# Sums over partitions of a matrix-vector product: eight TensorE products per group, or a transposing reduction on VectorE and four products at the end

## The reference

```python
ada = silu(c) @ w_ada + b_ada                      # (1, 1024) @ (1024, 6144)
sh_a, sc_a, g_a, sh_f, sc_f, g_f = split(ada, 6)
h = rmsnorm(x, norm_mix_w) * (1 + sc_a) + sh_a
h_res = x + g_a * token_mixer(h, ...)              # GLA + HGRN2, merged, @ w_out
h = rmsnorm(h_res, norm_ffn_w) * (1 + sc_f) + sh_f
h_res = h_res + g_f * conv_ffn(h, ...)             # @ w_up, 3-tap conv, silu*up, @ w_down
out = rmsnorm(h_res, final_norm_w)
```

## Time and profile before

| | us |
|---|---|
| median of 3 executions | 926.81 |
| lowest, highest | 925.79, 928.36 |
| the profiled execution, whole | 929.29 |
| its span, first to last instruction | 927.6 |
| TensorE busy in it | 897.6 |
| VectorE, ScalarE, GpSimd busy | 497.0, 456.5, 182.2 |

### The profile page before, as it was taken

The page is one execution under the profiler, slowest core; times in us unless marked ns, Lnnn a source line. Parts: engine busy times, 40 slices in busy tenths (PEclk is TensorE's granted clock), DMA queues, the critical chain, the costliest instruction groups (busy, mean ns, idle before and its releaser), DMA issues.

```text
span 927.6 us, 13516 instructions
## 1 busy us (share of the span) xinstructions
PE 897.6 (97%) x4828; PEld 743.4 (80%) x4828; DVE 497.0 (54%) x678; ACT 456.5 (49%) x699; POOL 182.2 (20%) x169
## 2 busy tenths in 40 slices
PE   5898999999999999999999989999999999999997
PEld 5776888888888888888887767888888888888885
DVE  2555873467634676346764357744454445623327
ACT  4475654656656565566655453533433333523224
POOL 2002253012531125311243000211112111100000
PEclk9899999999999999999999999999999999999999
DMA  9945452562425624256241940533333332232202
GB/s 326 352 141 153 118 158 64 165 182 69 115 66 160 181 68 113 78 148 184 65 128 31 203 138 10 150 90 98 105 91 90 99 104 91 98 130 90 91 0 92
DMA packets 146829, 112.16 MB, mean 121 GB/s; under 512 B 4493, under 2 KB 138137, under 8 KB 146537
## 3 DMA queue, kind: packets, MB, share of 16 engines
q1 hardware_dynamic: 146288, 111.37, 40.4%
q0 software_dynamic: 160, 0.20, 0.1%
q10 hardware_dynamic: 345, 0.13, 0.1%
HBM read 107.49 MB, written 4.20 MB: 120 GB/s over the span
## 4 chain that ended last, share of the span: by engine, by line
PE 89%; DVE 3%; issue 3%; DMA 2%; ACT 2%; POOL 1%; ACTq 0%; SPq 0%; POOLq 0%; DVEq 0%
PE ps L1341 27%; PE ps L1343 27%; PE ps L1342 26%; DMA hres<-xT_saved_dram 2%; PE ps L1478 1%; PE ps L1375 1%; PE ps L1480 1%; PE ps L1460 1%; PE ps L1429 1%; PE ps L1444 1%; DMA raw<-in_w_in_dram 1%; PE ps L1557 1%; PE ps L1447 1%; PE ps L1362 0%; DVE h_lo L1194 0%
## 5 line engine op out<-in xcount | busy, mean ns | idle before, releaser
L908 DVE TENSOR_TENSOR w_lo<-raw,w_hi 128x1024 fp32r<-128x1024 f32 x142 | 184.9, 1314 | 125.9 <-ACT w_hi L572 125.2
L1341 PE MATMUL ps<-h_hi,w_hi 128*128 128x512 f32 x608 | 238.5, 392 | 6.1 <-DVE h_lo L1258 3.3
L1343 PE MATMUL ps<-h_hi,w_lo 128*128 128x512 f32 x608 | 237.3, 390 | 0.0
L1342 PE MATMUL ps<-h_lo,w_hi 128*128 128x512 f32 x608 | 237.2, 390 | 0.0
L1341 PE MATMUL ps<-w_hi,h_hi 128*128 128x512 f32 x552 | 220.0, 399 | 3.8 <-DVE h_lo L948 3.8
L1343 PE MATMUL ps<-w_hi,h_lo 128*128 128x512 f32 x552 | 215.4, 390 | 0.0
L1342 PE MATMUL ps<-w_lo,h_hi 128*128 128x512 f32 x552 | 215.1, 390 | 0.0
L572 ACT ACTIVATE w_hi<-raw 128x1024 fp32r<-128x1024 f32 x142 | 146.9, 1052 | 75.2 <-PE ps L1343 48.8
L1341 PEld LDWEIGHTS ps<-h_hi,w_hi 128*128 128x128 f32 x608 | 114.5, 188 | 30.9 <-issue 5.2
L1342 PEld LDWEIGHTS ps<-h_lo,w_hi 128*128 128x128 f32 x608 | 114.6, 188 | 23.8 <-issue 0.2
L1343 PEld LDWEIGHTS ps<-h_hi,w_lo 128*128 128x128 f32 x608 | 114.5, 188 | 23.8
(11 more groups left out here) (209 smaller groups left out, 874.5 us busy)
## 6 DMA issues: line engine op xcount, KB each, us to landing
raw<-in_w_in_dram SPq DMA_DIRECT2D x68, 512.0 KB, 4.7
raw<-in_w_up_dram SPq DMA_DIRECT2D x44, 512.0 KB, 3.7
ada_w<-in_w_ada_dram SPq DMA_DIRECT2D x32, 512.0 KB, 4.1
raw<-in_w_down_dram SPq DMA_DIRECT2D x22, 512.0 KB, 3.3
ada_w<-in_w_ada_dram SPq DMA_DIRECT2D x8, 1024.0 KB, 8.7
raw<-in_w_out_dram SPq DMA_DIRECT2D x8, 512.0 KB, 4.3
x_tok<-in_x_dram SPq DMA_DIRECT2D x4, 512.0 KB, 5.1
w_first<-in_w_in_dram SPq DMA_DIRECT2D x8, 256.0 KB, 7.7
```

Of the source, the lines that this page charges most:

```text
L908: dve.tensor_tensor(w_lo[:, slot(u)].rearrange("p k c -> p (k c)"), raw[:, raw_slot(u)].rearrange("p k c -> p (k c)"), w_hi[:, slot(u)].re ...
L1341: pe.matmul(dst, a_hi, b_hi, start=start and i == 0, stop=False)
L1342: pe.matmul(dst, a_hi, b_lo, start=False, stop=False)
L1343: last = pe.matmul(dst, a_lo, b_hi, start=False, stop=stop and i == n - 1)
```

## The change

Three things are done in place of the eight products per group.

- Behind the eighth step of `ada_acc`, at n = 15 of each group, VectorE reduces it: `tensor_reduce` with `apply_transpose` turns each 32 x 32 block and sums what were its partitions. That leaves, for each quarter of the partitions, one sum per column, in 32 columns of a small tile `ada_t` that has room for all groups.
- A tile `stack` of 128 x 32, made once from the identity, has a one where p mod 32 is the column. In the output projection, right behind the last merged turn, four products with it add up the four quarters of all 128 columns and put the result on 32 partitions each.
- VectorE makes all 32 columns of `ada` in one addition, behind the two products of L1218. `ada_made` counts to 1 instead of 4. All that waited for it (the store to `gf_dram`, the scale `a_ffn`) waits for this one. `merged_turn` waits for it no more.

`squares`, a tile into which ScalarE writes values that nobody reads, now shares memory with `d_ref`, for room.

```diff
-        squares = sm("squares", [P, T])
+        squares = d_ref[:, 0]
...
+        stack = sm("stack", [P, 32])
+        ada_t = sm("ada_t", [P, GROUPS, 32])
...
                 if j == 5:
-                    sp.wait_ge(ada_made, GROUPS)
+                    sp.wait_ge(ada_made, 1)
                     sp.dma_start(gf_dram.rearrange("(k p) -> p k", p=P), ada[:, 40:48],
...
                 if m == 0:
-                    dve.wait_ge(ada_summed, g)
+                    dve.wait_ge(ada_folded, g)
...
+                if m == KT - 1:
+
+                    dve.wait_ge(ada_used, g * KT + KT)
+                    dve.tensor_reduce(ada_t[:, bass.ds(g, 1)].rearrange("p a b -> p (a b)"),
+                                      ada_acc[:].rearrange("p (b j) -> p b j", j=32),
+                                      mybir.AxisListType.X, ALU.add, apply_transpose=True).then_inc(ada_folded, 1)
...
                     if first and n == 7:
                         dve.wait_ge(nw_in, 32)
+                        dve.tensor_reduce(stack[:], ident[:].rearrange("p (b j) -> p j b", j=32),
+                                          mybir.AxisListType.X, ALU.add).then_inc(stack_made, 1)
...
-                    if n == 17:
-                        dve.wait_ge(ada_summed, g + 1)
-                        dve.tensor_tensor(ada[:, bass.ds(g * 8 + 16, 8)], ps[:, B_STATE + 1, 3 * P:3 * P + 8],
-                                          vecs[:, bass.ds(g * 8 + V_BADA + 16, 8)], ALU.add).then_inc(ada_made, 1)
...
                 dve.tensor_tensor(h_lo[:, k], ps[:, B_STATE + k - 6], h_hi[:, k].bitcast(F32), ALU.subtract
                                   ).then_inc(m_lo_made, 1)
+            dve.wait_ge(ada_summed, 1)
+            dve.tensor_tensor(ada[:, 16:48], ps[:, B_O, 0:32], vecs[:, V_BADA + 16:V_BADA + 48], ALU.add
+                              ).then_inc(ada_made, 1)
...
                 pe.wait_ge(state_made, (g + 1) * GROUP_STATES)
-                pe.wait_ge(ada_made, g + 1)
...
-                    if n == 16:
-
-                        pe.wait_ge(ada_used, g * KT + KT)
-                        pe.wait_ge(state_made, (g + 1) * GROUP_STATES)
-                        for m in range(KT):
-                            last = pe.matmul(ps[:, B_STATE + 1, 3 * P + m:3 * P + m + 1], ada_acc[:, m * P:(m + 1) * P],
-                                             ones[:, 0:1], start=True, stop=True)
-                        last.then_inc(ada_summed, 1)
...
+            def last_turn_and_ada():
+
+                merged_turn(GROUPS - 1)
+                pe.wait_ge(y_made, 12 * GROUPS)
+                pe.wait_ge(stack_made, 1)
+                pe.wait_ge(ada_folded, GROUPS)
+                for q in range(4):
+                    last = pe.matmul(ps[32 * q:32 * q + 32, B_O, 0:32], stack[:],
+                                     ada_t[:].rearrange("p g (m q) -> p (g m) q", q=4)[:, :, q], start=True, stop=True)
+                last.then_inc(ada_summed, 1)
...
-            interleaved(U_OUT, OUT_BANKS[:2], m_lo_made, M_LO, lambda k: merged_turn(GROUPS - 1) if k == 4 else None)
+            interleaved(U_OUT, OUT_BANKS[:2], m_lo_made, M_LO, lambda k: last_turn_and_ada() if k == 4 else None)
```

More of the change, by code:

```diff
@@ L282, in build @@
         ada0_made = sem("ada0_made")
+        stack_made = sem("stack_made")
+        ada_folded = sem("ada_folded")
         ada_summed = sem("ada_summed")
@@ L1219, in _ @@
                                   ).then_inc(m_lo_made, 1)
+            dve.wait_ge(ada_summed, 1)
+            dve.tensor_tensor(ada[:, 16:48], ps[:, B_O, 0:32], vecs[:, V_BADA + 16:V_BADA + 48], ALU.add
+                              ).then_inc(ada_made, 1)
             split_lo(U_OUT + 4, U_OUT + 5)
             split_lo(U_OUT + 5, U_OUT + 6)
-            dve.wait_ge(ada_made, GROUPS)
+            dve.wait_ge(ada_made, 1)
             dve.scalar_tensor_tensor(out=a_ffn, in0=ada[:, 32:40], scalar=1.0, in1=vecs[:, V_NFFN:V_NFFN + 8],
```

## The result

The changed kernel takes **931.74 us** (median of 6 runs, 930.27 to 934.92) against 926.79 us (6 runs, 925.79 to 931.24) for the kernel before: a ratio of 1.0048, 95% interval 1.003 to 1.0065. It is slower by 4.9 us, just clear of the 0.3% that counts as no change, and 1.1 us above the upper end of the predicted range. The forecast, 927.5 us and "the same", was wrong.

What follows compares the result with a forecast made beforehand. TensorE, busy 897.6 of 927.6 us, was taken as the bound. Terms -5.4 -0.1 +3.4 +1.4 +1.4 gave +0.7 us on the median 926.81: 927.5 us, "the same"; own ends 926 to 929.4, range with rivals 922.2 to 930.6.

Steps and rivals of the forecast that it cites:

- Groups 0 to 2: TensorE's column sums in the first three groups: removing them gains 1.8 us each, 5.4 us together.
- The last group: Sums ahead of the wait for `gate`: gain only 0.1 us, TensorE's stop grows from 1.7 to 3.5 us.
- The added operations: VectorE's reductions and `stack` cost nothing; four small TensorE products take 0.3 us (0 to 0.85), hidden by the `hres` wait.
- The moved store: Later `gf_dram` store on SyncE holds the `hres` load queued behind it: `hres` 3.4 us later, bounds 0 and 5.1.
- Rival 3: Slower: store takes its full 12.6 us again, both low-clock stretches lie wholly in matmuls; +3.6 us, 930.4 us, chance 0.13.
- The clock: TensorE at half speed behind the stops for `gate` and `hres`: 1.4 us lost at each, ends 0 and 2.0.
- the slower side: Whole kernel slower by over 0.3%: chance 0.13.

Runs made afterwards that it cites:

- experiments 1: Changed kernel without the 4 KB store to `gf_dram` (gate `g_f` left out, `gf_b` loaded from `final_norm_w`): 925.64 us, ratio 0.9973.
- experiments 2: Kernel before, with its store to `gf_dram` as late as in the changed one, right ahead of the `hres` load: 935.31 us, ratio 1.008.
- experiment 5: Changed kernel with the store to `gf_dram` behind the `hres` load and the projection's last loads, `gf_b`'s load later too: 925.35 us, ratio 0.9981.
- experiment 3: Kernel before without TensorE's column sums (`ada` lacks them), store and `hres` load untouched: 924.58 us, ratio 0.9967.
- experiment 4: Changed kernel with four unread 128x512 float32 products in TensorE's stop ahead of the output projection: 926.35 us, ratio 0.9995.
- k_two_fillers: Changed kernel with unread float32 products in two stops, four ahead of the output projection and five ahead of its unit 4: 927.74 us, ratio 0.9991.
- 6: Changed kernel with the store to `gf_dram` issued by GpSimd on its own queue, `hres` load still on SyncE's: 925.13 us, ratio 0.9976.
- both of 8: Changed kernel with half the store (512 four-byte values): 931.16 us, ratio 1.0041; or with the same 4 KB as 128 rows of 32 bytes: 925.65 us, ratio 0.9975.

## Why the prediction was wrong

By its own steps:

- **Groups 0 to 2, -5.4 us: right.** The period fell from 115.1 to 113.3 us.
- **The last group, -0.1 us: right in kind.** TensorE's stop was to grow to 3.5 us and grew to 4.0. In VectorE's timeline the six `h_lo` parts of that chain take longer than the 4.00 us of before:

```profile
491.29 4.50 DVE L1202 TENSOR_TENSOR h_lo<-merged,h_hi 128x384 fp32r<-128x384 f32 x6
```

  GpSimd is at work for 2.9 us of the 4.5, and was for 1.7 of the 4.0 before. That the two disturb each other I have not tested. All groups together gave 5.2 us, as the restart at 496.56 shows.
- **The added operations: right.** The reduction, 1.245 us, was covered; the small products took the 0.3 us that were chosen between 0 and 0.85. (The sixteen records of the sums are shown with 1.84 us, not 1.7, so the upper end should have been 0.92.)
- **The moved store: the mechanism right, the size too small.** Issued at 508.10, it held the load until it had landed, with an empty stretch in the traffic, as predicted; experiments 1, 2 and 5 show the hold from three sides. The prediction took 10.9 us for the store and 6.9 from its landing to the load's; the trace has 12.0 and 7.2. From the merged turn behind the projection's first units (the eight transpositions, at 504.99 now) to the landing of `hres` it was 17.5 us and is 22.35: **+4.8 us instead of +3.4**. The step that failed is what the prediction took to stay the same: "alone it should land 12.6 - 2.7 + 1.0 = 10.9 us after issue". Its first half was right: the store's first packet comes 0.9 us after the issue, instead of 2.5 behind the fresh weight load (in experiment 3, with such a load ahead, it is 2.5 again). But from the first packet to the landing it was 10.1 us before and 9.9 in experiment 3, where the `hres` load was issued 5 and 8 us behind it, and is 11.1 now, and 10.5 to 10.9 in experiments 2, 4 and `k_two_fillers`, where it follows at once. That is 1.1 us of the missing 1.4 (12.0 instead of 10.9); the other 0.3 is the 7.2 instead of 6.9. Whether it is the load right behind them that makes the writes slower was not tested. (The working has a slip besides: 506.85 + 4.3 is 511.15 and not "about 510". The traffic does end at 510, so the number was fit, the sum given for it was not.) Rival 3 was near in size, with the full 12.6, but not for its reason, "its time is that of the writes alone".
- **The clock, +1.4 +1.4 us: the step that failed by most.** The merged turn behind the first stop came 4.24 us sooner instead of 7.11, so that low stretch cost 2.9 us; the end of the projection's last unit came 3.03 us later where its fifth had restarted 0.58 us later, so the second cost 2.45. Together **5.3 us instead of 2.8**. I had taken the length of a low stretch from two places, 85 to 88 and 560 to 562.5, and put the end of each term at 2.0 us, where the two stretches measured lasted 6.8 us each. The same trace of before held a longer one that I hadn't read, at the start of the program:

```profile
23.70:30.30 6.60, 4.70 (x63) 3.75 (x67) 2.42 (x3) 1.89 (x4) 0.00 (x0) 0.50 1.07 380
```

  Half speed over 6.6 us would cost up to 3.3 us, and that should have been the end of each term. From 80 us on both lengths, 3.4 and 6.8 us, stand in the traces behind stops of 3.3 to 5.4 us, and once none (experiment 4). Even the stop of 4.0 us ahead of the projection has 6.8 us in the changed kernel and in experiment 5, and 3.4 in experiments 1, 6 and both of 8. What picks between them is open, so the 5.3 us are the sum of this execution, and another one of the same kernel may have less.

The sum as measured, with the 1.9 us of the start taken out: -5.2 (groups) + 2.9 (first low stretch) + 4.8 (`hres`) + 2.45 (second low stretch) - 0.25 (the rest, from the spans) = **+4.7 us**, beside the medians' +4.95. That it agrees so well is partly luck: it is one execution of each kernel, and executions of one kernel differ by more than that. The sign hung on the sizes. With the prediction's ends wide enough for what its own trace showed, +3.3 for a low stretch and +5.1 for the load, the slower side would have deserved more than 0.13, and the range would have reached 926.8 - 5.5 + 5.1 + 3.3 + 3.3 = 933 us. The ends that the prediction did give were not added up either: they come to 921.3 (no hold, no low clock) and 930.4 us, not to 926 and 929.4. Rival 3 had the shape of what came (+3.6 predicted): its 5.1 for the load is near the 4.8 measured, its 4.0 for the clock falls short of 5.3.

The two losses aren't independent of the gain. Both of the stops that cost the clock are made of time that the change saved ahead of a chain or moved behind one; experiment 3 shows it without the store, where 7.2 us less work on a busy TensorE bring 2.8.

## What to carry to other kernels

When an edit moves the moment at which a small scattered store becomes ready, look at every transfer issued behind it, whichever queue it is on: put the store behind the loads that someone waits for, or give it a form in which each row is contiguous. Where an edit shortens work ahead of a chain that doesn't move, the gain turns into a stop, and on a busy TensorE the stop can have a price of its own in clock (here those of 3.3 us and more did, with one exception, and those of 1.0 and 1.7 us did not): price it from the longest low stretch in the whole trace, and try a few unread matmuls in the stop, which here lengthened nothing that the traces show. A term near the sign's turning point deserves ends from the worst row, not from the two nearest.

## What the runs showed of the hardware that I had not expected

- A store of 1024 values of four bytes, scattered, lands 11.4 to 12.6 us after its issue, and 13.1 to 14.2 where it went out behind the 2 MB load or on GpSimd's queue; half of it 11.0; the same 4 KB as 128 rows of 32 bytes 1.4. The Trainium skill ("DMA: Bandwidth & Descriptors", section "Specifications") has transfers under 512 B done as read-modify-write; the rows of 32 bytes are under it too and are fast, so that rule alone doesn't tell the two forms apart.
- Such a store holds a 2 MB load right behind it on its queue (17 to 19 us instead of 8 to 9): the load's first sixteen packets stand for up to 11.1 us. It slows a load on another queue that was issued 0.4 us ahead of it (13.6). The Trainium skill ("DMA: Bandwidth & Descriptors", section "Two DMAs through the same engine are not ordered") lets a later transfer complete first; in no run here did the load land ahead of a scattered store that was issued before it.
- Behind stops of 4.0 and 5.4 us TensorE had, in the changed kernel, half its clock for 6.8 us, counted from inside the stop. In the four traces with four unread 128x512 products ahead of the projection the clock stayed at 1.00 there, and in all seven with this stop of 4 us and without them it fell to 0.50. Five at the second stop and four at the third were tried once each, with the clock at 1.00 too.
